# Tile-by-tile halves, a longer head step and moved splits in a transformer kernel in fp32

## The chip, the core and the metric

The kernel runs on one core of one Trainium2 chip. The metric is the device time of one execution in microseconds (us). Engines: PE is TensorE (matmuls and transposes), DVE is VectorE, ACT is ScalarE, POOL is GpSimd, SP is SyncE, which issues the weight loads. Each engine has its own queue and works through it strictly in order; semaphores tie the queues together.

## What is computed

Two transformer layers follow one another on 256 tokens of width 2048, all in fp32:

```python
# first layer: mixer, cross attention, feed-forward
h = rmsnorm(x, g); dq, dk, dv, rq, rk, rv, rg = split_cols(h @ w_in)
da = rmsnorm(diff_attention(dq, dk, dv, lam, slopes)) * (1 - lam_init)   # 4 heads
ret = rmsnorm(retention(rq, rk, rv)) * silu(rg)
x = x + concat(da, ret) @ w_o
xo = softmax((rmsnorm(x) @ w_xq) (rmsnorm(mem) @ w_xk)^T / sqrt(512)) @ (rmsnorm(mem) @ w_xv)   # 4 heads
x = x + xo @ w_xo
hf = rmsnorm(x);  x = x + (silu(hf @ w_gate) * (hf @ w_up)) @ w_down
x = rmsnorm(x, norm_f_g)
# second layer: modulated input, windowed GQA and pooling branches, gated merge
shift, scale, gate = split(silu(c) @ w_ada + b_ada)
h = rmsnorm(x) * (1 + scale) + shift
q, k, v, gate_a, u, gate_p = split(h @ w_in_2)
merged = g_a * (y_a @ w_branch_attn) + g_p * (y_p @ w_branch_pool)
out = x + gate * rmsnorm(merged @ w_out)
```

## The kernel before

**Operands.** Tokens stand in two tiles of 128 (tile 0 and tile 1). Each fp32 factor is split into a high and a low part in fp32r, and each product is three matmuls, high by high, high by low and low by high, of 128 rows by 512 columns (L1069 to L1071). Weights come in *half panels*: 256 rows by 512 columns, in SBUF as 128 x 1024 numbers. SP loads one into one of eight raw places, ACT makes its high part whi (L1604), DVE its low part wlo (L2334: raw minus whi). Both lie in a ring of four slots (HALVES), slot n % 4. A *step* of the stream is one half panel met with one tile (6 matmuls) or with both (12). Panels are computed in pairs, whose first chunk is done with seven products in the manner of Strassen (M1 to M7); this needs sums of raw halves (L2347) and sums of activations, the *forms* (fah, fal, fbh, fbl).

**Order.** The class Stream lists the steps of the whole program; each of the four programs (tensor, scalar, vector, gpsimd) goes through the same list. Ahead of each step ACT and DVE make the parts of the halves up to `made`, which is four past the last half that has been met; after it a queue of *jobs*, Python generators, goes on by one `yield` of its first job. So the order of the other work (attention heads, norms, splits of activations) against the matmuls is written out by these yields and by `pause(n)`.

**Differential heads.** On TensorE a head is scores (L704, L705), then a turn of the probabilities and probabilities times v (L719 to L721), which end in bank A[0]. ACT squares the result (L1100), DVE makes the mean (L1653), POOL the root (L2389), and DVE scales the result (L1890). After the scale comes the next head's scores or, behind the pair's second head, the turn of the mixed rows (L648). One yield lies between the last matmul of a head and what follows it.

**hx3 and memory.** While w_o's last panels run, the memory rows are squared on ACT (mem_stats, L1100, eight squares in four steps), and hx3, the last chunk of the cross attention's input, is turned by TensorE (L648) and split (ACT L1113, DVE L1674).

**xq and xo.** The cross heads wait for c_p (DVE) and for turned copies (L1758, L1181). The forms of xo are built by DVE (L1703 to L1706, L1710) and ACT (L1157) while xq's last panels run. L1165 on ACT scales a panel's rows by a root before TensorE turns them (L648).

**e3 and kv.** e3 is the last panel of the last down projection, with six halves: the first two are met with both tiles, the last four with tile 0 and then with tile 1 ("last"), so that tile 0's sum is complete four halves before tile 1's. kv is the first panel of the second layer, with eight: its first four halves are met with tile 0, then tile 1, and the last four with both ("first"). In between stands the final norm: for each tile DVE adds the residual (L2050), multiplies by the gain (L2052), makes the mean (L2054 to L2062); ACT makes two squares (L1100); POOL makes the roots (L2389). Then each chunk j of tile t is scaled by the root (scale_chunk: DVE L2043 for even j, ACT L1374 for odd), turned by TensorE (L836), modulated by scale and shift (ACT L1407, DVE L2085), and split (ACT L1413, DVE L2090). kv's eight low parts are made not by DVE but by POOL (low_parts, L2406), counted by the semaphore lo_pool. The chunks come in the order (0,0), (1,0) behind tile 0 and (0,1), (1,1), (2,0), (2,1), (3,0), (3,1) behind tile 1, each in banks ps4 and ps5.

## Time and profile before

| | |
|---|---|
| median of 3 runs | 2101.16 us (2100.3 to 2101.31) |
| profiled execution, its own time | 2102.25 us |
| its span, first to last instruction | 2100.5 us |
| mean granted TensorE clock | 0.997 |
| PE busy | 2062.7 us (98%) |
| DVE busy | 1678.4 us (80%) |
| ACT busy | 1175.9 us (56%) |
| POOL busy | 73.0 us (3%) |

A row of a timeline gives start, length, engine, line, operation and shape, and in brackets how long the engine had been idle and what released it. Matmuls overlap, since the next one is issued before the last has ended; what a matmul costs is read from start to start, not from its length. The page's idle time is the end of one to the start of the next, so an excess from start to start is some 0.15 us more than the idle time in brackets.

### The profile page before, as it was taken

The page shows a single profiled execution, that of the slowest core. Times are in us where ns is not written, and L with a number is a line of the kernel's source. Part 1 is how long each engine was busy: PE and PEld are TensorE (multiplying, and loading weights), DVE is VectorE, ACT ScalarE, POOL GpSimd, SP SyncE. Part 2 cuts the span into 40 slices and gives each one's busy share as a digit, 9 for nine tenths or more (in the row PEclk, how much of TensorE's full clock was granted, in tenths as well). Part 3 has the DMA queues.
Part 4 walks back from the last instruction along what each step waited for, and adds up shares of the span by engine and source line. Part 5 has one row for each costly group of instructions (what it writes and reads, how often), then busy time and mean ns, then how long its engine had stood idle before and what let it go on. Part 6 is the DMA issues. An engine that isn't in the chain of part 4 may idle for free.

```text
span 2100.5 us, 25386 instructions
## 1 busy us (share of the span) xinstructions
PE 2062.7 (98%) x9334; PEld 1700.3 (81%) x9334; DVE 1678.4 (80%) x1839; ACT 1175.9 (56%) x1522; POOL 73.0 (3%) x94
## 2 busy tenths in 40 slices
PE   9999999999999999999999999999899999999998
PEld 8887888788887888888888888888678888888786
DVE  6777778876765788998889898898688768988875
ACT  7665556755654565555555555555656655654453
POOL 1000000000000000000000000000310000000000
PEclk9999999999999999999999999999999999999999
DMA  9555557565544458777777777776465566889653
GB/s 343 171 177 170 184 172 261 188 200 179 189 161 150 140 191 289 255 262 248 235 239 256 264 240 248 234 275 204 125 208 181 181 191 226 266 290 325 222 198 107
DMA packets 218955, 453.75 MB, mean 216 GB/s; under 512 B 14400, under 2 KB 16592, under 8 KB 218704
## 3 DMA queue, kind: packets, MB, share of 16 engines
q1 hardware_dynamic: 212928, 432.07, 61.4%
q0 software_dynamic: 5616, 19.94, 3.0%
q8 instruction: 74, 1.21, 0.2%
q14 instruction: 49, 0.40, 0.1%
q10 hardware_dynamic: 288, 0.13, 0.0%
HBM read 447.88 MB, written 4.19 MB: 215 GB/s over the span
## 4 chain that ended last, share of the span: by engine, by line
PE 85%; issue 7%; DVE 5%; ACT 2%; DMA 1%; POOL 0%; DVEq 0%; ACTq 0%; POOLq 0%
PE ps L1069 26%; PE ps L1071 26%; PE ps L1070 26%; DVE wlo L2334 2%; PE ps L648 2%; PE ps L778 1%; PE ps L798 1%; ACT whi L1604 0%; ACT junk L1100 0%; PE ps L884 0%; DMA FR<-in_mem_dram 0%; PE ps L926 0%; PE ps L915 0%; PE ps L864 0%; DVE raw L2347 0%
## 5 line engine op out<-in xcount | busy, mean ns | idle before, releaser
L2334 DVE TENSOR_TENSOR wlo<-raw,whi 128x1024 fp32r<-128x1024 f32 x832 | 1006.0, 1220 | 261.1 <-ACT whi L1604 254.0
L1604 ACT ACTIVATE whi<-raw 128x1024 fp32r<-128x1024 f32 x840 | 882.2, 1058 | 592.6 <-PE ps L1071 545.9
L1069 PE MATMUL ps<-whi,ah 128*128 128x512 f32 x1618 | 642.6, 397 | 7.9 <-DVE wlo L2334 4.1
L1071 PE MATMUL ps<-whi,al 128*128 128x512 f32 x1618 | 631.7, 390 | 0.0
L1070 PE MATMUL ps<-wlo,ah 128*128 128x512 f32 x1618 | 630.7, 390 | 0.0
L1069 PEld LDWEIGHTS ps<-whi,ah 128*128 128x128 f32 x1618 | 304.5, 188 | 72.6 <-issue 6.9
L1071 PEld LDWEIGHTS ps<-whi,al 128*128 128x128 f32 x1618 | 304.1, 188 | 64.8
L1070 PEld LDWEIGHTS ps<-wlo,ah 128*128 128x128 f32 x1618 | 304.7, 188 | 61.2 <-issue 0.2
L1069 PE MATMUL ps<-whi,bh 128*128 128x512 f32 x862 | 341.2, 396 | 5.7 <-DVE wlo L2334 4.0
L1071 PE MATMUL ps<-whi,bl 128*128 128x512 f32 x862 | 336.1, 390 | 0.0
L1070 PE MATMUL ps<-wlo,bh 128*128 128x512 f32 x862 | 335.6, 389 | 0.0
L2347 DVE TENSOR_TENSOR raw<-raw 128x1024 f32<-128x1024 f32 x160 | 197.9, 1237 | 26.7 <-DVE wlo L2334 26.7
L1069 PEld LDWEIGHTS ps<-whi,bh 128*128 128x128 f32 x862 | 161.9, 188 | 41.6 <-issue 4.6
L1071 PEld LDWEIGHTS ps<-whi,bl 128*128 128x128 f32 x862 | 161.8, 188 | 34.3
L1070 PEld LDWEIGHTS ps<-wlo,bh 128*128 128x128 f32 x862 | 162.0, 188 | 33.5 <-issue 1.0
L1985 DVE SCALAR_TENSOR_TENSOR FR<-raw,Z,FR 128x1024 f32<-128x1024 f32 x90 | 115.0, 1278 | 0.0
L1069 PE MATMUL ps<-whi,fah 128*128 128x512 f32 x208 | 84.0, 404 | 0.5 <-DVE fal L1710 0.5
L1071 PE MATMUL ps<-whi,fal 128*128 128x512 f32 x208 | 81.2, 390 | 0.0
L1070 PE MATMUL ps<-wlo,fah 128*128 128x512 f32 x208 | 81.1, 390 | 0.0
L1176 ACT ACTIVATE side<-ps 128x512 f32<-128x512 f32 x120 | 70.8, 590 | 17.7 <-PE ps L1071 17.7
L2389 POOL TENSOR_TENSOR Z<-Z 128x2 f32<-128x2 f32 (+1 forms) x18 | 13.1, 729 | 1443.5 <-DVE Z L1653 770.4
L1715 DVE TENSOR_TENSOR FR<-ps,side 128x512 f32<-128x512 f32 x81 | 53.1, 683 | 7.5 <-PE ps L1071 7.5
(237 smaller groups left out, 1340.3 us busy)
## 6 DMA issues: line engine op xcount, KB each, us to landing
raw<-in_w_in_dram SPq DMA_DIRECT2D x168, 512.0 KB, 4.5
raw<-in_w_ada_dram SPq DMA_DIRECT2D x96, 512.0 KB, 4.7
raw<-in_w_gate_dram SPq DMA_DIRECT2D x88, 512.0 KB, 4.9
raw<-in_w_up_dram SPq DMA_DIRECT2D x88, 512.0 KB, 5.2
raw<-in_w_down_dram SPq DMA_DIRECT2D x88, 512.0 KB, 5.3
raw<-in_w_merge_dram SPq DMA_DIRECT2D x64, 512.0 KB, 5.1
raw<-in_w_o_dram SPq DMA_DIRECT2D x32, 512.0 KB, 4.8
raw<-in_w_xk_dram SPq DMA_DIRECT2D x32, 512.0 KB, 4.7
```

What stands on the lines that cost most here:

```text
L648: ins = e.transpose(T[b].ap[:, kk * 256 + t * 128:kk * 256 + t * 128 + 128], src[:, t, (2 * b + kk) * 128:(2 * b + kk + 1) * 128], ident[: ...
L778: ins = e.matmul(A[0].ap[:, t * S:(t + 1) * S], QTC[:, d, t * 128:(t + 1) * 128], XKT[:, 4 * h + d, :], start=(d == 0), stop=(d == 3))
L798: ins = e.matmul(A[b].ap[:, dd * S:(dd + 1) * S], XV[:, k, c0:c0 + 128], PTC[:, k, :], start=(k == 0), stop=(k == 1))
L1069: e.matmul(o, xh[:, k, tokens], wh, start=first, stop=False, skip_group_check=more)
L1070: e.matmul(o, xh[:, k, tokens], wl, start=False, stop=False, skip_group_check=more)
L1071: ins = e.matmul(o, xl[:, k, tokens], wh, start=False, skip_group_check=more, stop=kk == 1 and (st.end or st.form in READ))
L1176: done(e.activation(side_of(pair[place[0]], place[1]), bank_of(pair[panel], t)[:, :], ACT.Copy), "snap")
L1604: done(e.activation(whi[:, n % HALVES, :], place(item), ACT.Copy), "hi")
L1715: return e.tensor_tensor(dst, src, side_of(p, t), side_op(p))
L1985: done(e.scalar_tensor_tensor(acc, src, csilu[:, k:k + 1], acc, ALU.mult, ALU.add), "ada")
L2334: done(e.tensor_tensor(wlo[:, n % HALVES, :], src, whi[:, n % HALVES, :].bitcast(F32), ALU.subtract), "lo")
L2347: done(e.tensor_tensor(place(item), place(add), place(item), ALU.subtract if minus else ALU.add), "t_sum")
```

## The change

Four parts.

1. e3 and kv are met tile by tile in six halves each instead of four: all of e3's six by tile, kv's first six by tile and its last two with both. A ring of four cannot hold six, so two halves lie aside: e3's first two in the places of chunks 2 and 3 of activations that are free then, kv's first two in the places of the forms. `_slots` works out the slot of each half, what it waits for, and `made`. POOL's low parts go to DVE, and lo_pool is gone. The chunks come as (0,0), (1,0), (2,0), (0,1), (1,1), (2,1), (3,1), (3,0), by turns in the banks T (ps4, ps5) and A (ps6, ps7); (0,0) and (1,0) are turned while e3 still runs for tile 1. On ACT and DVE a job second_input does tile 0's chunks, tile 1's gain product and squares, and then the rest, with a chunk's high and low parts one step behind its modulation from (0,1) on. The sum for M5 of the pair behind kv comes one half nearer to its use.
2. diff_head has one more yield on TensorE, ACT and DVE at its end.
3. hx3 is split before the last memory squares: on ACT after the second of the four steps of squares, on DVE after two pauses, on TensorE two steps earlier.
4. xo's forms take one step more on TensorE, ACT and DVE, and the third cross head pauses two steps instead of three ahead of its turn, as the fourth has done.

```diff
                 if c == 1 and panel.kind in ("ba", "bp"):
                     self._add_ada(self._late)
                 self._entry(self._item(p, c, hf))
-        if panel.stagger == "first":
-            self.pool_halves = range(base, base + n)
-        a, b = {"first": (0, HALVES), "last": (n - HALVES, n), None: (n, n)}[panel.stagger]
+        for h, at in {("e", 3): ((0, ("a", 2)), (1, ("a", 3))),
+                      ("kv", 0): ((0, "forms_a"), (1, "forms_b"))}.get((panel.kind, panel.i), ()):
+            self.aside_at[base + h] = at
+        by_tile = HALVES + sum(base <= m for m in self.aside_at)
+        a, b = {"first": (0, by_tile), "last": (n - by_tile, n), None: (n, n)}[panel.stagger]
...
+        early = 1 if self.panels[f - 1].stagger == "first" else 2
+        for form, n in (("M5", at["M5"] - early), ("M6", at["M3"] + 1), ("M7", at["M1"] + 2),
...
+        self.slot, self.slot_free, ring = {}, {}, []
+        for n in range(self.total):
+            if n in self.aside_at:
+                self.slot[n], self.slot_free[n] = self.aside_at[n], self.free[n]
+            else:
+                self.slot[n] = len(ring) % HALVES
+                self.slot_free[n] = ring[-HALVES] + 1 if len(ring) >= HALVES else 0
+                ring.append(n)
+        first_use = {}
+        for i, st in enumerate(self.steps):
+            first_use.setdefault(st.n, i)
+        met = made = 0
+        for i, st in enumerate(self.steps):
+            ahead = len(self.steps)
+            if len(st.tiles) == 1 and st.form is None:
+                ahead = HALVES if self.panels[st.p].kind == "out" else 3
+            while made < self.total and self.slot_free[made] <= met and (
+                    made in self.aside_at or first_use[made] <= i + ahead):
+                made += 1
+            self.steps[i] = st._replace(made=made)
+            if st.taken:
+                met = st.n + 1
...
+        mod_order = ((0, 0), (1, 0), (2, 0), (0, 1), (1, 1), (2, 1), (3, 1), (3, 0))
...
+        def mod_banks(j, t):
+            return A if mod_order.index((j, t)) % 2 else T
...
+        def split_at(n):
+            at_n = stream.slot[n]
+            if isinstance(at_n, int):
+                return whi[:, at_n, :], wlo[:, at_n, :]
+            if isinstance(at_n, tuple):
+                parts = [buf[:, 4 * at_n[1]:4 * at_n[1] + 4, :] for buf in at[at_n[0]]]
+            else:
+                parts = [buf[:, :, :] for buf in forms[at_n[-1]]]
+            return [part.rearrange("p a b -> p (a b)") for part in parts]
...
                 e.matmul(A[0].ap[:, 256:512], AAT[:, 256:384], vb[:, 1, cols], start=False,
                          stop=True).then_inc(A[0].full, 1)
                 yield
+                yield
...
-                for _ in range(3 if h < 3 else 2):
+                for _ in range(3 if h < 2 else 2):
...
+                        jobs.start(make_forms(3))
...
+                    if t == 0:
+                        jobs.start(pause(3))
+                        for j, tt in mod_order:
+                            jobs.start(modulated(j, tt))
+                            if (j, tt) in ((1, 0), (2, 0)):
+                                jobs.start(pause(2 if j == 1 else 1))
+                    else:
...
-                        jobs.start(pause(4))
+                        jobs.start(pause(2))
...
                     for t in range(2):
                         square(MT[j % 2][:, t, :], ss_m[:, 2 * j + t:2 * j + t + 1], "m_sq")
                     yield
+                    if j == 1:
+                        yield from turn_x("hx3", ("hx", 3), gcols("nx", 3))
...
+            def second_input():
+                yield from pause(3)
+                mod_sums(0, 0)
+                mod_high(0, 0)
+                yield
+                mod_sums(1, 0)
+                mod_high(1, 0)
+                yield
+                yield
+                gain_square(1)
+                yield
+                mod_sums(2, 0)
+                mod_high(2, 0)
+                yield
+                scale_chunk(1, 1)
+                yield
+                for i, (j, t) in enumerate(mod_order[3:]):
+                    for nj, nt in mod_order[5 + i:6 + i]:
+                        if nj % 2:
+                            scale_chunk(nj, nt)
+                    mod_sums(j, t)
+                    if i:
+                        mod_high(*mod_order[2 + i])
+                    yield
+                mod_high(*mod_order[-1])
...
                 elif kind == "e" and i < 3:
                     aside.start(down2(p, i))
                 elif kind == "e":
-                    last_down(p, t)
+                    down_square(p, t)
+                    if t == 0:
+                        gain_square(t)
+                        scale_chunk(1, t)
+                        jobs.start(second_input())
+                    else:
+                        jobs.start(make_forms("mod"))
+                        jobs.start(pause(4))
...
                         jobs.start(make_forms("mem"))
                     if c == 3:
                         jobs.start(mem_stats())
-                        jobs.start(turn_x("hx3", ("hx", 3), gcols("nx", 3)))
...
                 a11, a21, a12, a22 = (AF[name][:, 2 * k:2 * k + 2, t * P:(t + 1) * P] for k in range(2) for t in range(2))
                 after_own(done(e.tensor_tensor(a22, a21, a22, ALU.subtract)))
                 after_own(done(e.tensor_tensor(a21, a11, a21, ALU.subtract)))
+                if name == "xo":
+                    yield
...
                 yield
             def mem_stats():
-                for _ in range(4):
-                    yield
+                yield from pause(2)
+                yield from to_stationary("hx3", ("hx", 3), gcols("nx", 3))
+                yield from pause(2)
                 e.wait_ge(s["m_sq"], 8)
...
+            def mod_low(j, t):
                 e.wait_ge(s["mod_hi"], mod_order.index((j, t)) + 1)
                 hi, lo = (part[:, :, t * P:(t + 1) * P] for part in hi_lo(("mod", j)))
-                done(e.tensor_tensor(lo, tmp, hi.bitcast(F32), ALU.subtract), f"mod{t}")
+                done(e.tensor_tensor(lo, tmp_of(j, t), hi.bitcast(F32), ALU.subtract), f"mod{t}")
+            def second_input(p):
+                yield from pause(3)
+                scale_chunk(2, 0)
+                mod_sums(0, 0)
+                yield
+                mod_low(0, 0)
+                mod_sums(1, 0)
+                yield
+                mod_low(1, 0)
+                yield
+                down_gain(p, 1)
+                yield
+                down_mean(1)
+                mod_sums(2, 0)
+                mod_low(2, 0)
+                yield
+                scale_chunk(0, 1)
+                yield
+                for i, (j, t) in enumerate(mod_order[3:]):
+                    for nj, nt in mod_order[5 + i:6 + i]:
+                        if nj % 2 == 0:
+                            scale_chunk(nj, nt)
+                    mod_sums(j, t)
+                    if i:
+                        mod_low(*mod_order[2 + i])
+                    yield
+                mod_low(*mod_order[-1])
...
-            def low_parts(upto):
-                while made[0] < upto:
-                    n = stream.pool_halves[made[0]]
-                    made[0] += 1
-                    src = place(stream.entries[n].item)
-                    e.wait_ge(s["hi"], n + 1)
-                    e.tensor_tensor(wlo[:, n % HALVES, :], src, whi[:, n % HALVES, :].bitcast(F32),
-                                    ALU.subtract).then_inc(s["lo_pool"], 1)
...
             final_roots(0)
-            low_parts(4)
             final_roots(1)
-            low_parts(8)
```

In the excerpts below the names are those of the kernel's buffers: ps a PSUM bank, FR a scratch region, Z the small columns, X the residual, ah and al the high and low parts of activations. The lines of the changed kernel differ from those before: L1113 to L1115 are the three matmuls, L743 and L744 the scores, L1144 the square, L1157 the high split of a turned chunk, L1679 whi, L2440 wlo, L2127 and L2131 tile 1's sum and gain product, L2162 a modulated chunk's low part, L2155 its modulation, L2122 the scale by the root.

TensorE at the second pair of differential heads, before: six matmuls of the pair's forms product stand behind the head's L721 (just above), then come the scores of head 3.

```order
L1069 MATMUL ps<-whi,fah 128x512
L1070 MATMUL ps<-wlo,fah 128x512
L1071 MATMUL ps<-whi,fal 128x512
L704 MATMUL ps<-FR 128x128 [waits s_a0_free]
L705 MATMUL ps<-FR 128x256
L704 MATMUL ps<-FR 128x128 [waits s_a1_free]
L705 MATMUL ps<-FR 128x256
L1069 MATMUL ps<-whi,ah 128x512 [waits s_ev10,s_lo]
L1070 MATMUL ps<-wlo,ah 128x512
L1071 MATMUL ps<-whi,al 128x512
```

And after: the same six come first, and these six of the next step follow them ahead of the scores.

```order
L1113 MATMUL ps<-whi,ah 128x512 [waits s_ev10,s_lo]
L1114 MATMUL ps<-wlo,ah 128x512
L1115 MATMUL ps<-whi,al 128x512
L1113 MATMUL ps<-whi,ah 128x512
L1114 MATMUL ps<-wlo,ah 128x512
L1115 MATMUL ps<-whi,al 128x512
L743 MATMUL ps<-FR 128x128 [waits s_a0_free]
L744 MATMUL ps<-FR 128x256
L743 MATMUL ps<-FR 128x128 [waits s_a1_free]
L744 MATMUL ps<-FR 128x256
```

The scores moved by one step of 6 matmuls, from behind the product with fah to behind the next one.

ACT at the end of w_o, before: whi parts, the memory squares of chunks 2 and 3, and then hx3's high split.

```order
L1604 ACTIVATE whi<-raw 128x1024 [waits s_half,s_raw7]
L1100 ACTIVATE junk,Z<-FR 128x512 [waits s_m_sq,s_mt0]
L1100 ACTIVATE junk,Z<-FR 128x512 [waits s_m_sq]
L1604 ACTIVATE whi<-raw 128x1024 [waits s_half,s_t_sum]
L1100 ACTIVATE junk,Z<-FR 128x512 [waits s_m_sq,s_mt1]
L1100 ACTIVATE junk,Z<-FR 128x512 [waits s_m_sq]
L1604 ACTIVATE whi<-raw 128x1024 [waits s_half,s_raw2]
L1113 ACTIVATE ah<-ps,G 128x256 [waits s_half,s_t0_full]
L1113 ACTIVATE ah<-ps,G 128x256
```

And after: hx3's split (L1157) stands ahead of those squares.

```order
L1679 ACTIVATE whi<-raw 128x1024 [waits s_half,s_raw7]
L1157 ACTIVATE ah<-ps,G 128x256 [waits s_half,s_t0_full]
L1157 ACTIVATE ah<-ps,G 128x256
L1679 ACTIVATE whi<-raw 128x1024 [waits s_half,s_t_sum]
L1157 ACTIVATE ah<-ps,G 128x256 [waits s_t1_full]
L1157 ACTIVATE ah<-ps,G 128x256
L1679 ACTIVATE whi<-raw 128x1024 [waits s_half,s_raw2]
L1144 ACTIVATE junk,Z<-FR 128x512 [waits s_m_sq,s_mt0]
L1144 ACTIVATE junk,Z<-FR 128x512 [waits s_m_sq]
```

hx3's four pieces moved up by two steps and the squares of two chunks down by two.

DVE where e3's second tile ends, before: the low parts of chunks (0,0) and (1,0), then tile 1's sum, gain product and mean with no weight work in between (POOL has it).

```order
L2090 TENSOR_TENSOR al<-FR,ah 128x4x128 [waits s_mod_hi]
L2085 TENSOR_SCALAR FR<-ps,Z 128x128 [waits s_t1_full]
L2085 TENSOR_SCALAR FR<-ps,Z 128x128
L2090 TENSOR_TENSOR al<-FR,ah 128x4x128 [waits s_mod_hi]
L2050 TENSOR_TENSOR FR<-ps,X 128x512 [waits s_half]
L2052 TENSOR_TENSOR X<-FR 128x512 [waits s_ev11]
L2054 TENSOR_REDUCE Z<-Z 128x1 [waits s_sqg]
L2056 TENSOR_REDUCE Z<-Z 128x1 [waits s_sqf]
L2057 TENSOR_SCALAR Z<-Z 128x1 [waits s_dve]
L2058 SCALAR_TENSOR_TENSOR Z<-Z 128x1 [waits s_dve]
L2061 TENSOR_TENSOR Z<-Z 128x1 [waits s_sqg,s_dve]
L2062 TENSOR_SCALAR Z<-Z 128x1 [waits s_dve]
```

And after: weight low parts stand between the low part of (1,0), tile 1's sum and its gain product.

```order
L2440 TENSOR_TENSOR wlo<-raw,whi 128x1024 [waits s_hi]
L2162 TENSOR_TENSOR al<-FR,ah 128x4x128 [waits s_mod_hi]
L2127 TENSOR_TENSOR FR<-ps,X 128x512 [waits s_half]
L2440 TENSOR_TENSOR wlo<-raw,whi 128x1024 [waits s_hi]
L2131 TENSOR_TENSOR X<-FR 128x512 [waits s_ev11]
L2440 TENSOR_TENSOR wlo<-raw,whi 128x1024 [waits s_hi]
L2136 TENSOR_REDUCE Z<-Z 128x1 [waits s_sqg]
L2138 TENSOR_REDUCE Z<-Z 128x1 [waits s_sqf]
L2139 TENSOR_SCALAR Z<-Z 128x1 [waits s_dve]
L2140 SCALAR_TENSOR_TENSOR Z<-Z 128x1 [waits s_dve]
L2143 TENSOR_TENSOR Z<-Z 128x1 [waits s_sqg,s_dve]
L2144 TENSOR_SCALAR Z<-Z 128x1 [waits s_dve]
```

Behind the mean stand, in the changed order, a chunk of tile 0 and one more weight part, and then the scale of (0,1), the first L2122 here.

```order
L2155 TENSOR_SCALAR FR<-ps,Z 128x128 [waits s_t1_full]
L2155 TENSOR_SCALAR FR<-ps,Z 128x128
L2162 TENSOR_TENSOR al<-FR,ah 128x4x128 [waits s_mod_hi]
L2440 TENSOR_TENSOR wlo<-raw,whi 128x1024 [waits s_hi]
L2122 TENSOR_SCALAR FR<-X,Z 128x512 [waits s_r]
L2122 TENSOR_SCALAR FR<-X,Z 128x512 [waits s_a1_full,s_r]
L2155 TENSOR_SCALAR FR<-ps,Z 128x128 [waits s_a1_full]
```

Three, then four, low parts of weights moved in ahead of that scale, and so did the modulation of (2,0); before, the scale of (0,1) stood right behind the mean.

## Rows read from the trace of the kernel before

**Rows 1.** Waits of TensorE over the span: in all, times, longest (us).

```profile
PE ps L1069 <- POOL wlo L2406: 1.8, 2, 1.2
```

**Rows 2.** Timeline, TensorE, 655 to 660: start, us, engine, line, operation [idle before, releaser].

```profile
655.46 0.39 PE L1070 MATMUL ps<-wlo,ah 128*128 128x512 f32 x1
655.69 0.39 PE L1071 MATMUL ps<-whi,al 128*128 128x512 f32 x1
658.25 1.97 PE L648 MATMUL ps<-ident,FR 128*128 128x128 f32 x8 [2.18 <-ACT FR L1165]
```

**Rows 3.** Timeline, TensorE, at the heads and the turns behind them.

```profile
90.36 0.49 PE L704 MATMUL ps<-FR 128*128 128x128 f32 x2 [0.24 <-DVE FR L1890]
...
165.09 0.49 PE L704 MATMUL ps<-FR 128*128 128x128 f32 x2 [1.58 <-DVE FR L1890]
...
182.21 0.66 PE L648 MATMUL ps<-ident,FR 128*128 128x128 f32 x4 [1.58 <-DVE FR L1890]
...
189.93 0.66 PE L648 MATMUL ps<-ident,FR 128*128 128x128 f32 x4 [1.09 <-ACT FR L1165]
```

**Rows 4.** Timeline, TensorE, at 416.

```profile
416.00 0.47 PE L1069 MATMUL ps<-whi,bh 128*128 128x512 f32 x1 [1.60 <-DVE wlo L2334]
```

**Rows 5.** Timeline, TensorE, from the end of e3 into kv.

```profile
1496.36 0.63 PE L836 MATMUL ps<-ident,FR 128*128 128x128 f32 x4 [0.82 <-issue]
1497.70 0.50 PE L1069 MATMUL ps<-whi,ah 128*128 128x512 f32 x1 [0.71 <-DVE al L2090]
...
1507.07 0.66 PE L836 MATMUL ps<-ident,FR 128*128 128x128 f32 x4 [2.60 <-DVE FR L2043]
...
1508.44 0.63 PE L1069 MATMUL ps<-whi,ah 128*128 128x512 f32 x1
1508.87 0.63 PE L1070 MATMUL ps<-wlo,ah 128*128 128x512 f32 x1
...
1509.72 1.05 PE L836 MATMUL ps<-ident,FR 128*128 128x128 f32 x4
```

**Rows 6.** Timeline, TensorE, after kv, in the q pair.

```profile
1533.17 0.50 PE L1069 MATMUL ps<-whi,fah 128*128 128x512 f32 x1 [0.46 <-DVE fal L1710]
...
1537.45 0.47 PE L1069 MATMUL ps<-whi,ah 128*128 128x512 f32 x1 [1.27 <-DVE wlo L2334]
```

**Rows 7.** Timeline, VectorE, before the scores at 165.09.

```profile
164.16 0.88 DVE L1890 TENSOR_SCALAR FR<-ps,Z 128x256 f32<-128x256 f32 x2 [0.80 <-POOL Z L2389]
```

**Rows 8.** Timeline, ScalarE, at the memory squares.

```profile
409.74 0.63 ACT L1100 ACTIVATE junk<-FR 128x512 bf16<-128x512 f32 x1 [3.84 <-DMA FR<-in_mem_dram]
```

**Rows 9.** Timeline, GpSimd, in kv.

```profile
1494.70 10.78 POOL L2406 TENSOR_TENSOR wlo<-raw,whi 128x1024 fp32r<-128x1024 f32 x4 [1.23 <-ACT whi L1604]
```

**Rows 10.** Timeline, VectorE, 1501 to 1508.

```profile
1501.09 2.15 DVE L2052 TENSOR_TENSOR X<-FR 128x512 f32<-128x512 f32 x1
...
1503.59 1.90 DVE L2058 SCALAR_TENSOR_TENSOR Z<-Z 128x1 f32<-128x1 f32 x1
...
1507.77 0.73 DVE L2085 TENSOR_SCALAR FR<-ps,Z 128x128 f32<-128x128 f32 x2 [0.36 <-PE ps L836]
```

**Rows 11.** Page, part 5: count | busy us, mean ns | idle before.

```profile
L2334 DVE TENSOR_TENSOR wlo<-raw,whi 128x1024 fp32r<-128x1024 f32 x832 | 1006.0, 1220 | 261.1 <-ACT whi L1604 254.0
L1604 ACT ACTIVATE whi<-raw 128x1024 fp32r<-128x1024 f32 x840 | 882.2, 1058 | 592.6 <-PE ps L1071 545.9
```

**Rows 12.** Groups of VectorE, 1478 to 1550: count | busy us, mean ns.

```profile
L2043 DVE TENSOR_SCALAR FR<-X,Z 128x512 f32<-128x512 f32 x4 | 1.8, 484 | 1.3 <-POOL Z L2389 1.3
L2050 DVE TENSOR_TENSOR FR<-ps,X 128x512 f32<-128x512 f32 x2 | 1.4, 686 | 1.7 <-PE ps L1071 1.7
```

**Rows 13.** Groups of ScalarE, 1478 to 1550: count | busy us, mean ns.

```profile
L1413 ACT ACTIVATE ah<-FR 128x512 fp32r<-128x512 f32 x8 | 5.1, 631 | 4.6 <-issue 3.7 <-ACT FR L1407 0.7
```

**Rows 14.** Windows: length, busy us and count by engine, PEclk, DMA share, GB/s.

```profile
656.00:662.00 6.00, 3.82 (x15) 3.37 (x15) 4.24 (x6) 2.88 (x4) 0.00 (x0) 0.72 0.53 175
1520.00:1550.00 30.00, 26.62 (x116) 20.73 (x115) 28.60 (x32) 17.25 (x22) 10.26 (x11) 1.00 0.55 173
```

167 lines of the change are left out of this document (70 added, 97 removed).

## Prediction

> **What bounds the kernel now.** I read the busy times first: TensorE works in 98% of the span, and its work is 8400 matmuls of 512 columns that the change neither adds to nor removes. So only the time in which TensorE stands still, or runs at a low clock, can move. Second I read its waits over the whole span [rows 1] and third, in its timeline, each place where one start follows the last by more than the work explains. Fed without a break, a 512-column matmul starts every 0.23 us (655.46 to 655.69) [rows 2], so a half panel met with one tile (6 matmuls) is 1.36 us and with both tiles 2.72 us. The change touches places that together hold about 25 us of such excess. These are the places:
> - pair 0 and 1 of the differential heads: gaps of 0.24, 1.58, 1.58 and 1.09 us [rows 3], in starts an excess of 0.40, 1.75, 1.75 and 1.25 us;
> - 416.00, TensorE idle 1.60 us for a low part [rows 4];
> - 658.25, idle 2.18 us [rows 2];
> - the stretch from the down projection's last panel (e3) to the first of the second layer (kv), with eleven waits from 1496.36 to 1548.08 that sum to 12.6 us in starts, the first two, the largest and two of the last in [rows 5, 6], and a low clock after the largest.
>
> Of the clock, rows show this: after the 2.60 us of idle before 1507.07 the matmuls at 1508.44 and 1508.87 stand 0.43 apart, its lower level (1.2 GHz; at 2.4 GHz 0.23), until about 1511.4, which costs about 2 us [rows 5]. After the 2.18 us before 658.25 [rows 2] the mean granted clock of 656 to 662 is 0.72 [rows 14], which costs about 1.6 us. After gaps of 1.6 us it doesn't.
>
> **Differential heads.** One more step between the heads' last matmul and the means puts the scores of the next head, or the turn of the result, behind 12 matmuls and not 6 (at mix 0: 12 and not 24, since there the head ends one step later while the turn stays). The chain behind is fixed: square, mean, root, then DVE's two L1890 (0.88 us) [rows 7]. Where 6 matmuls left 1.75 us, 12 leave 1.75 - 1.36 = 0.40. By place: 90.36 loses its 0.40, mix 0 gains a new 0.40; 165.09 goes from 1.75 to 0.40; 182.21 now has 24 matmuls ahead and loses 1.75; 189.93 loses 1.25. Net **-4.35 us**. Bounds: -3.6 if the new gap at mix 0 is as large as the one now at 189.93, -5.1 if the 0.40s aren't there. The added step queues no DMA and each engine's rows between are whi and wlo parts with slack at that point.
>
> **hx3 ahead of the memory squares.** At 416.00 DVE's low part is late because ACT's high part is, and ACT stood still 3.84 us at 409.74 for the memory rows' DMA [rows 8], then did two squares per step. With the split of hx3 (two 0.42 us pieces and no DMA behind it) in front and squares later, the high part for that step comes without two squares (4 instructions, 1.5 us) ahead of it. The 1.85 us goes: **-1.85 us**, bounds -2.2 (with the wait's shadow after it) and -1.0 (if the split, whose transposes PE makes at 413.80, is itself late by the step that was saved). The memory mean comes later too, but its root is first read when xk is scaled, a panel on; if that weren't so, the cost would be a step's wait there, which is within the bound of -1.0.
>
> **xq and xo.** The forms of xo take one step more on each engine and the third cross head pauses one less, so that the turn of its panel stands one step later. At 658.25 TensorE waits for ACT's L1165, which waits behind DVE's forms and L1715 in the order. A step more is 2.72 us, more than the 2.18 idle. The wait (2.34 in starts) and the low clock after it (1.6) go, less a slack of 0.15 that is missing on the c_p link: **-3.8 us**. Bounds: -2.3 if a smaller idle time still lowers the clock, -3.9 in full.
>
> **e3 and kv.** Here more is exchanged than saved, and it decides the size of the result. Now: POOL makes kv's eight low parts, four in 10.78 us [rows 9], and TensorE waits for two of them, 1.8 us [rows 1]; beside them the product of tile 1 with the gain takes 2.15 us (an undisturbed one of its shape 0.69 [rows 12]) and a one-column instruction 1.90 [rows 10], some 7 us of lengthening in all up to 1530. After: DVE makes them, 8 x 1.22 = 9.8 us more [rows 11], and gets the 7 back. I walked the order of the changed kernel with undisturbed durations: low part 1.22, high part 1.06 (0.95 apart), sum or product of 512 columns 0.69, scale 0.48 [rows 12], square 0.63 [rows 8] and its read 0.19, ScalarE's high part of a chunk 0.63 [rows 13], half a chunk's modulation 0.73 [rows 10].
> - Tile 0's sum comes three us earlier (1486.3 and not 1489.3), because six halves are met tile by tile; both first chunks are then turned inside tile 1's matmuls. The waits at 1496.36 and 1497.70 (0.99 + 0.96) go. kv starts at 1495.6 and not 1497.7, and its first two halves lie ready.
> - Then DVE and ACT work in strict turns, each step needing the other's last: half 2's high part to 1497.0, its low part to 1498.25 (TensorE waits 0.4), chunk (1,0)'s low part to 1498.9, tile 1's sum to 1499.5, its square, half 3's high part to 1501.2, its low part to 1502.45: TensorE, which needs it at 1500.2, waits **2.2**. The gain product to 1503.05, its square, half 4's parts to 1504.8 and 1506.0, the mean's six small rows to 1507.0, chunk (2,0)'s sums, high and low part to 1509.2, half 5's low part to 1510.65, and only then the scale of chunk (0,1), to 1511.1. TensorE has finished half 3 at 1503.9 and stands **7.2 us**; a low clock of about 1.7 follows, as at 1507.07.
> - So (0,1) is turned at 1511.1, not 1507.07: 4.0 us later, with one half (1.36) and one chunk's turn (0.41) more already done. From there to the first step of the q pair, before 78 matmuls (17.7), six turns (2.5), low clock (2.0), waits (3.8): 26.1, the row at 1533.17 [rows 6]. After: 72 matmuls (16.4), five turns (2.1), low clock (1.7), waits (1.1): 21.2, so about 1532.3. DVE's lighter work after it takes another 0.4 off the waits at 1537.45 and 1548.08 [rows 6].
>
> Net **-1.3 us**; bounds +2 (each of the nine hand-overs 0.3 longer than the bare rows) and -6 (whi and wlo parts overlapping better than my walk). What POOL held up on DVE is taken as gone in full because the last lengthened instruction, a one-column one from 1503.59 on, ended at 1505.49 as POOL's fourth did at 1505.48 [rows 9, 10]. The Trainium skill, SBUF — State Buffer, section "Who interferes with whom", says that a DVE instruction with two SBUF inputs and a GpSimd instruction reading SBUF take turns on an exclusive port pair, and the loser blocks; by it nothing of the lengthening can stay, and if another cause held it (the loads landing) up to 2 us of the 7 would remain on DVE at 1521. The Trainium skill, Perfetto Trace Analysis, section "Optimizing Scalar/DVE Operations", would speak against the move, since there DVE is the busy one: 28.60 of 30 us in 1520 to 1550 [rows 14]; by it the sum would be worse by at most 9.8 - 7 = 2.8 us, which takes -1.3 to +1.5, inside the bounds.
>
> **The sum.** -4.35 - 1.85 - 3.8 - 1.3 = -11.3 us against the profiled execution's 2102.25, so 2090.95. That execution lies 1.09 above the median 2101.16; the same for the changed kernel gives **2089.9 us**. What a measurement can tell from no change is 0.2%, 4.2 us: 2097.0 and 2105.4 are the bounds of "same".
>
> **Rivals.**
> - *The turns between DVE and ACT don't bind.* If high parts run ahead (ACT is idle much of 1496 to 1511) and my strict order is wrong about which row waits, the 7.2 us stall and its low clock shrink to nothing: 2089.9 - 8.9 = 2081. Against it: each wait stands in the changed order.
> - *A step later is a step too late.* In heads, hx3 or xo the moved work meets the next deadline: one gap like 658.25's with its low clock (3.9) comes back, or hx3 pays its full 1.85 and the head gaps half: 2094 to 2097. For it: the 2.72 step covers xo's gap by only 0.5 us.
> - *Slower: tile 1's chunks go at round-trip pace.* After (0,1), four more chunk turns stand between half panels, one every 6 matmuls (1.77 us with the turn). A chunk's round (modulation 0.73, low part 0.69, scale 0.48, ACT's high part 0.63, the low part of a half 1.22) is 3.75 us, with hand-overs 4.0, if nothing of it overlaps, which gives 4 x 2.2 = 8.9 us of waits, and TensorE, idle more than half of it, would keep its lower level for the 48 matmuls that kv meets by tile from there (48 x 0.2 - 1.7 = 7.9 more): 2089.9 + 8.9 + 7.9 = 2106.7. It decides from a round of 3.7 us with that clock, of 5.6 without. Against it: banks alternate in twos and the rows 1507.07 to 1512 show two such turns 2.65 apart [rows 5].
> - *POOL's work was free and DVE's isn't* is the 2.8 us above, within the forecast.
>
> **Chances.** Forecast (2086 to 2094) 0.60; turns don't bind (2079 to 2086) 0.14; step too late (2094 to 2098) 0.21, a quarter of it within 0.2%; slower 0.03; the rest, 0.02, in between. So faster 0.90, same 0.07, slower 0.03. The range reaches from the first rival's 2081 to 2096, which leaves out about 0.05 below and 0.1 above.
>
> **What would show it.** In the profile after: no idle at 164 to 190 above 0.5 us; none at the step after hx3's turn; at xo no low clock; no POOL tensor work at e3; the gain product of tile 1 at 0.69; tile 0's end three us earlier against the kernel's start of e3; a 2 us wait at kv's half 3 and a wait of about 7 us for DVE's scale at the turn of (0,1), with slow matmuls after. Wrong would be the forecast if that last wait is under 4 us, or if any second one above 2 us follows.

## The result and the profile after

The changed kernel takes **2090.92 us** (median of 5 runs, 2090.46 to 2090.99) against 2100.58 us for the kernel before (5 runs, 2100.12 to 2101.31): 9.66 us less, a ratio of 0.9953 with a 95% interval of 0.9938 to 0.9967, so 7 to 13 us. The forecast was 2089.9 us, which was 11.3 us less than the median before. The profiled execution took 2090.46 us, 11.8 less than the profiled one before.

First part 1 of the changed kernel's page: busy time, share of the span and count of instructions by engine. POOL's work fell from 73.0 to 53.4 us, and DVE's stayed at 1678, although it took over eight low parts.

```profile
span 2088.3 us, 25390 instructions
...
PE 2058.2 (99%) x9334; PEld 1699.1 (81%) x9334; DVE 1678.3 (80%) x1847; ACT 1175.1 (56%) x1522; POOL 53.4 (3%) x86
```

TensorE runs the same 9334 instructions in both kernels, so the two traces can be laid over each other: the start of the same place in TensorE's queue, after minus before. The third column is what each stretch changed. Each trace is one execution.

| place (start in the trace before) | after - before, us | stretch | forecast |
|---|---|---|---|
| 84, ahead of the heads | -0.36 | -0.36 | 0 |
| 264, behind the heads | -4.89 | -4.53 | -4.35 |
| 403, ahead of the memory squares | -4.92 | -0.03 | 0 |
| 423, behind hx3 | -6.35 | -1.43 | -1.85 |
| 631, ahead of the cross heads | -6.37 | -0.02 | 0 |
| 711, behind xo's first turn | -10.30 | -3.93 | -3.8 |
| 1478, start of e3 | -10.21 | +0.09 | 0 |
| 1548, in the q pair | -11.44 | -1.23 | -1.3 |
| 1982 | -11.48 | -0.04 | 0 |
| 1990, last panels | -12.05 | -0.57 | 0 |

Two of these stretches, the first and the last, don't belong to the change, as the second profile of the kernel before shows below.

Three places in TensorE's timeline of the changed kernel: the turn at mix 0, the scores at head 3 (165.09 in [rows 3]) and the turn behind hx3. In brackets: idle time and releaser.

```profile
116.15 0.66 PE L688 MATMUL ps<-ident,FR 128*128 128x128 f32 x4 [0.21 <-DVE FR L1967]
...
164.66 0.49 PE L743 MATMUL ps<-FR 128*128 128x128 f32 x2 [0.21 <-DVE FR L1967]
...
416.87 0.66 PE L688 MATMUL ps<-ident,FR 128*128 128x128 f32 x4 [0.75 <-ACT FR L1211]
```

The new gap at mix 0 and the rest at head 3 are 0.21 us each (0.37 in starts, forecast 0.40). What stood at 90.36, 182.21 and 189.93 in [rows 3] is gone. At 416.87 a wait has grown: 0.91 in starts, where the trace before has 0.30.

TensorE's timeline of the changed kernel from kv's half 3 (1492.10) over the turn of chunk (0,1) (1500.51) to half 4, which answers to [rows 5]:

```profile
1492.10 0.50 PE L1113 MATMUL ps<-whi,ah 128*128 128x512 f32 x1 [1.90 <-DVE wlo L2440]
...
1500.51 1.11 PE L877 MATMUL ps<-ident,FR 128*128 128x128 f32 x4 [6.47 <-DVE FR L2122]
1501.28 0.78 PE L1113 MATMUL ps<-whi,ah 128*128 128x512 f32 x1
1501.85 0.63 PE L1114 MATMUL ps<-wlo,ah 128*128 128x512 f32 x1
1502.28 0.63 PE L1115 MATMUL ps<-whi,al 128*128 128x512 f32 x1
```

Both waits of the forecast are there: 2.07 us in starts (forecast 2.2) and 6.87 (7.2), and then matmuls 0.43 apart. VectorE's timeline beside it, from the low part of (1,0) to the scale of (0,1):

```profile
1487.80 0.68 DVE L2162 TENSOR_TENSOR al<-FR,ah 128x512 fp32r<-128x512 f32 x1
1488.40 0.68 DVE L2127 TENSOR_TENSOR FR<-ps,X 128x512 f32<-128x512 f32 x1
1490.82 1.22 DVE L2440 TENSOR_TENSOR wlo<-raw,whi 128x1024 fp32r<-128x1024 f32 x1 [1.74 <-ACT whi L1679]
1491.97 0.68 DVE L2131 TENSOR_TENSOR X<-FR 128x512 f32<-128x512 f32 x1
1494.39 1.23 DVE L2440 TENSOR_TENSOR wlo<-raw,whi 128x1024 fp32r<-128x1024 f32 x1 [1.74 <-ACT whi L1679]
...
1496.42 0.72 DVE L2155 TENSOR_SCALAR FR<-ps,Z 128x128 f32<-128x128 f32 x2
1497.89 0.69 DVE L2162 TENSOR_TENSOR al<-FR,ah 128x512 fp32r<-128x512 f32 x1 [0.74 <-ACT ah L1453]
1498.83 1.23 DVE L2440 TENSOR_TENSOR wlo<-raw,whi 128x1024 fp32r<-128x1024 f32 x1 [0.25 <-ACT whi L1679]
1499.97 0.88 DVE L2122 TENSOR_SCALAR FR<-X,Z 128x512 f32<-128x512 f32 x2
```

And ScalarE's, at the same time (L1144 is tile 1's square, L1679 the high part of a half):

```profile
1489.12 0.63 ACT L1144 ACTIVATE junk<-FR 128x512 bf16<-128x512 f32 x1 [2.50 <-DVE FR L2127]
...
1489.75 1.04 ACT L1679 ACTIVATE whi<-raw 128x1024 fp32r<-128x1024 f32 x1
1492.68 0.63 ACT L1144 ACTIVATE junk<-X 128x512 bf16<-128x512 f32 x1 [1.89 <-DVE X L2131]
...
1493.31 1.04 ACT L1679 ACTIVATE whi<-raw 128x1024 fp32r<-128x1024 f32 x1
```

Read the brackets of both from top to bottom. Twice DVE stands 1.74 us for a high part of ACT, and ACT had stood 2.50 and 1.89 us for the row of DVE just above (the sum, then the gain product), on which its square waits; the high part stands behind the square. In the 12.2 us from 1487.80 to 1499.97 DVE is idle 4.5, and both of TensorE's waits end on a row of DVE. The gain product takes 0.68 us, where [rows 10] had 2.15.

### The profile page after: what moved, and what is told of

Its sections match the earlier page's. It is cut to its first block and busy times, and to the rows that moved or that the text cites. A ratio compares the mean times of both kernels' runs of the same rounds, so it can differ in the third digit from the quotient of the medians.

```text
span 2088.3 us, 25390 instructions
## 1 busy us (share of the span) xinstructions
PE 2058.2 (99%) x9334; PEld 1699.1 (81%) x9334; DVE 1678.3 (80%) x1847; ACT 1175.1 (56%) x1522; POOL 53.4 (3%) x86
## 5 line engine op out<-in xcount | busy, mean ns | idle before, releaser
L2440 DVE TENSOR_TENSOR wlo<-raw,whi 128x1024 fp32r<-128x1024 f32 x836 | 1010.9, 1221 | 258.1 <-ACT whi L1679 250.9
L1679 ACT ACTIVATE whi<-raw 128x1024 fp32r<-128x1024 f32 x836 | 877.9, 1058 | 583.7 <-PE ps L1115 541.1
L1113 PE MATMUL ps<-whi,ah 128*128 128x512 f32 x1610 | 638.7, 397 | 6.7 <-DVE wlo L2440 6.5
L1115 PE MATMUL ps<-whi,al 128*128 128x512 f32 x1610 | 628.2, 390 | 0.0
L1113 PEld LDWEIGHTS ps<-whi,ah 128*128 128x128 f32 x1610 | 302.7, 188 | 70.3 <-DVE wlo L2440 5.1
L1115 PEld LDWEIGHTS ps<-whi,al 128*128 128x128 f32 x1610 | 302.5, 188 | 64.4
L1113 PE MATMUL ps<-whi,bh 128*128 128x512 f32 x854 | 337.9, 396 | 4.1 <-DVE wlo L2440 2.4
L1115 PE MATMUL ps<-whi,bl 128*128 128x512 f32 x854 | 332.9, 390 | 0.0
L1113 PEld LDWEIGHTS ps<-whi,bh 128*128 128x128 f32 x854 | 160.4, 188 | 38.6 <-issue 4.9
L1115 PEld LDWEIGHTS ps<-whi,bl 128*128 128x128 f32 x854 | 160.3, 188 | 34.1
L1113 PE MATMUL ps<-whi,fah 128*128 128x512 f32 x208 | 84.0, 404 | 0.0
L1115 PE MATMUL ps<-whi,fal 128*128 128x512 f32 x208 | 81.2, 390 | 0.0
```

The lines of the kernel that those rows point to most:

```text
L1113: e.matmul(o, xh[:, k, tokens], wh, start=first, stop=False, skip_group_check=more)
L1115: ins = e.matmul(o, xl[:, k, tokens], wh, start=False, skip_group_check=more, stop=kk == 1 and (st.end or st.form in READ))
L1679: done(e.activation(split_at(n)[0], place(item), ACT.Copy), "hi")
L2440: done(e.tensor_tensor(lo, place(stream.entries[n].item), hi.bitcast(F32), ALU.subtract), "lo")
```

## The experiments

**Each part alone.** Four kernels hold one part of the change each. The heads:

```diff
                 e.matmul(A[0].ap[:, 256:512], AAT[:, 256:384], vb[:, 1, cols], start=False,
                          stop=True).then_inc(A[0].full, 1)
                 yield
+                yield
...
                     square(A[0].ap[:, q * 256:q * 256 + 256], ss_d[h][:, q:q + 1], "d_sq")
                 yield
+                yield
...
                                           root_col[f"d{h}"][:, q:q + 1], None, ALU.mult)
                 ins.then_inc(A[0].free, 1)
                 yield
+                yield
```

> The kernel before with one more yield at the end of each differential head on TensorE, ACT and DVE, and nothing else. If the four waits at the heads and turns behave as summed: -4.35 us against the kernel before (-3.6 to -5.1). Rival, that the moved scores only meet the next deadline: -1 to -2.5.

Measured: 2096.02 us (10 runs) beside 2100.17 (31 runs of the kernel before on the same chip), 4.15 less, ratio 0.9981 (0.9972 to 0.9991). In its trace the stretch from 84 to 264 is 4.6 us shorter. The added step does what the sum said.

hx3 alone (first TensorE's pause, then ACT, then DVE):

```diff
                     if c == 3:
-                        jobs.start(pause(4))
+                        jobs.start(pause(2))
...
                     yield
+                    if j == 1:
+                        yield from turn_x("hx3", ("hx", 3), gcols("nx", 3))
...
                         jobs.start(mem_stats())
-                        jobs.start(turn_x("hx3", ("hx", 3), gcols("nx", 3)))
...
             def mem_stats():
-                for _ in range(4):
-                    yield
+                yield from pause(2)
+                yield from to_stationary("hx3", ("hx", 3), gcols("nx", 3))
+                yield from pause(2)
...
                         jobs.start(mem_stats())
-                        jobs.start(to_stationary("hx3", ("hx", 3), gcols("nx", 3)))
```

> The kernel before with only hx3's split ahead of the last memory squares. As summed: -1.85 us. The trace of the changed kernel holds a new wait of 0.91 in starts where 0.30 was, at the turn at 416.87: if that is this part's doing, -1.4. Rival: the new wait comes from another part, then -1.85.

Measured: 2099.31 us, 0.86 less, ratio 0.9993 (0.9984 to 1.0002), which isn't clear of no change by its interval. Its trace is 1.4 us shorter between 403 and 423 and has the wait of 0.90 at the turn (421.41). So that wait is this part's doing, the first of the two cases expected: ACT's scale for the turn stands behind DVE's rows, and the step that was saved brings TensorE there earlier.

xq and xo alone (excerpt: ACT has the same shorter pause, and DVE one at its c_p loop):

```diff
-            def make_forms():
-                yield
-                yield
+            def make_forms(steps=2):
+                yield from pause(steps)
...
-                for _ in range(3 if h < 3 else 2):
+                for _ in range(3 if h < 2 else 2):
...
                     if i == 1:
-                        jobs.start(make_forms())
+                        jobs.start(make_forms(3))
...
                     done(ins, "af")
                 yield
+                if name == "xo":
+                    yield
```

> The kernel before with only the extra step of xo's forms and the third cross head's shorter pause. -3.8 us, of which about 2.3 is the wait at 658.25 and 1.6 the low clock behind it. Rival, that a shorter wait stays and still lowers the clock: -2.3 or less.

Measured: 2097.15 us, 3.02 less, ratio 0.9988 (0.9978 to 0.9997), so 0.6 to 4.6 us: between the two, and the interval holds both. Its trace against the trace before is 3.90 shorter from 631 to 711, as in the changed kernel. What can make the median give less is shown further down. The extra step and the shorter pause were not taken apart.

e3 and kv alone, which is the changed kernel with the other three parts put back:

> The changed kernel without its other three parts: only e3 and kv in six halves by tile, low parts on DVE, chunks in the new order. -1.3 us against the kernel before (+2 to -6). If the parts are independent, the four runs add up to the whole change's -9.7.

Measured: 2100.3 us, 0.13 more, ratio 0.9998 (0.9989 to 1.0007). So the median shows no gain from the largest part of the diff. Its trace repeats both waits (2.05 and 6.9 us in starts). The four runs add up to 7.9 us and not 9.7; the difference lies inside their intervals and isn't explained further.

**What makes the wait of 6.87 us.** Four kernels move work on DVE and ACT in the stretch around it. The kernels before that ran beside them have medians of 2100.57 and 2100.35, the one beside the changed kernel 2100.58, so differences from the changed kernel below 0.3 us mean nothing. The first changes DVE's order only:

```diff
                 down_mean(1)
+                scale_chunk(0, 1)
                 mod_sums(2, 0)
                 mod_low(2, 0)
                 yield
-                scale_chunk(0, 1)
                 yield
```

> The changed kernel with DVE's scale of chunk (0,1) directly behind tile 1's mean, ahead of the modulation of (2,0) and of half 5's low part. If DVE's order is what TensorE waits for at that turn (6.87 us in starts), the turn comes 2.4 us sooner and a new wait of about 1.5 us for the low part of (2,0) follows at half 4: -0.5 to -2 us against the changed kernel, 2089 to 2090.4. Rival, that what counts is the sum of DVE's work and not its order: no change, 2090.9.

Measured: 2090.29 us (2090.01 to 2090.79, 4 runs; the kernel before beside it 2100.57), 0.6 less than the changed kernel's 2090.92. TensorE's timeline:

```profile
1497.76 0.69 PE L877 MATMUL ps<-ident,FR 128*128 128x128 f32 x4 [3.93 <-DVE FR L2122]
...
1499.83 0.79 PE L1113 MATMUL ps<-whi,ah 128*128 128x512 f32 x1 [1.39 <-DVE al L2162]
```

The turn comes 2.75 us sooner. About half of that is given back at once, at half 4, to the low part of (2,0), which now ends last: 1.66 in starts. Nearly all of the rest goes to the clock. Behind that wait it is low until 1505.08, over ten matmuls and a turn; behind the long wait of the changed kernel it is low over one turn and five matmuls.

```profile
1502.00:1505.00 3.00, 3.00 (x10) 2.41 (x10) 1.45 (x4) 1.78 (x4) 0.00 (x0) 0.50 0.65 175
```

The turn two further on starts at 1505.57, and at 1505.63 in the changed kernel. From e3's start to 1548 the two traces differ by 0.2 us, so of the 0.6 us between the medians no more than that is seen in them. DVE's order is what TensorE waits for at that turn, but one row alone only moves the wait on.

The second gives tile 1's norm to DVE and ACT in one piece:

```diff
 # DVE, where tile 1's sum stands
                     else:
+                        down_gain(p, 1)
+                        down_mean(1)
                         jobs.start(make_forms("mod"))
...
 # DVE, second_input
-                down_gain(p, 1)
-                yield
-                down_mean(1)
-                mod_sums(2, 0)
-                mod_low(2, 0)
-                yield
                 scale_chunk(0, 1)
+                mod_sums(2, 0)
+                yield
+                mod_low(2, 0)
+                yield
                 yield
...
 # ACT, where tile 1's square stands
                     else:
+                        gain_square(1)
                         jobs.start(make_forms("mod"))
...
 # ACT, second_input
-                gain_square(1)
-                yield
                 mod_sums(2, 0)
+                yield
                 mod_high(2, 0)
-                yield
                 scale_chunk(1, 1)
                 yield
+                yield
```

> The changed kernel with tile 1's norm in one piece: on DVE sum, gain product and mean without weight low parts in between, on ACT both squares together, and the scale of (0,1) and the modulation of (2,0) one step sooner. If the strict turns between ACT and DVE make the long wait: the wait at half 3 grows from 2.1 to 2.8, the one of 6.87 at the turn of (0,1) goes with the low clock behind it, and one of about 1.2 comes at half 4: -6.5 us against the changed kernel, about 2084.4 (2083 to 2087). Rival, that ACT's and DVE's total work bounds this stretch: within 1 us of 2090.9.

Measured: **2084.54 us** (2084.45 to 2084.73, 4 runs), 6.4 us less than the changed kernel, ratio to the kernel before 0.9925 (0.9908 to 0.9941). Its TensorE timeline over the same places:

```profile
1492.99 0.50 PE L1113 MATMUL ps<-whi,ah 128*128 128x512 f32 x1 [2.73 <-DVE wlo L2440]
...
1494.64 1.06 PE L877 MATMUL ps<-ident,FR 128*128 128x128 f32 x4
1495.76 0.79 PE L1113 MATMUL ps<-whi,ah 128*128 128x512 f32 x1
```

The turn of (0,1) follows half 3 without a wait, at 1494.64 and not 1500.51. This settles the cause: the same instructions, no fewer on any engine, in another order. The total came out as expected, but two of its terms did not: the low clock did not go (3.4 us of it from 1494.29 on, behind the longer wait at half 3), and the wait expected at half 4 was 0.35 us in starts and not 1.2. How much of the 6.4 us is due to the norm in one piece and how much to the scale and modulation one step sooner was not taken apart; the kernel above shows that the sooner scale alone brings almost nothing.

The third lets the parts of halves met by tile be made up to four steps ahead, on top of the second:

```diff
-                ahead = HALVES if self.panels[st.p].kind == "out" else 3
+                ahead = HALVES
```

> The changed kernel with tile 1's norm in one piece and, besides, ScalarE's and VectorE's parts of halves met by tile made up to four steps ahead instead of three. If DVE's work in 1484 to 1497 is what bounds now: within 1 us of the version with the norm in one piece (2084.5), a smaller wait at half 3 and a new one of 2 to 3 at the turn of (0,1). Rival, that the late high parts of ACT are the bound: 2082 or less.

Measured: 2087.77 us (2086.48 to 2088.39, 4 runs), 3.2 us worse than without it, so neither side was right. Its waits by the timeline:

```profile
1486.70 0.51 PE L1113 MATMUL ps<-fah,ah 128*128 128x512 f32 x1 [1.12 <-DVE al L2162]
...
1490.86 0.50 PE L1113 MATMUL ps<-whi,ah 128*128 128x512 f32 x1 [0.72 <-DVE al L2162]
...
1495.64 0.66 PE L877 MATMUL ps<-ident,FR 128*128 128x128 f32 x4 [1.76 <-DVE FR L2122]
...
1498.02 0.80 PE L1113 MATMUL ps<-whi,ah 128*128 128x512 f32 x1 [1.72 <-DVE al L2162]
```

I had looked at the waits from half 3 on only (the two lower rows, about 2 us each in starts) and had left out the upper two (1.30 and 0.97); half 3 itself has no wait any more. Low parts of weights that are made sooner stand in front of the chunks' own low parts, which TensorE needs first. And from 1498 to 1503 the granted clock is 0.50:

```profile
1498.00:1503.00 5.00, 4.98 (x14) 4.03 (x15) 1.96 (x6) 2.44 (x6) 0.00 (x0) 0.50 0.41 129
```

The last puts half 3's parts where both engines wait anyway, on top of the second:

```diff
 # ACT, ahead of tile 1's squares
+                    if t == 1:
+                        make(made + 1)
                     down_square(p, t)
...
 # DVE
                         down_gain(p, 1)
+                        make(made + 1)
                         down_mean(1)
...
-                scale_chunk(0, 1)
                 mod_sums(2, 0)
+                scale_chunk(0, 1)
```

> As the version with the norm in one piece, but half 3's high part goes ahead of tile 1's squares on ACT and its low part between the gain product and the mean on DVE. The wait at half 3 falls from 2.9 to about 0.9, one of about 1.2 comes at the turn of (0,1) and one of about 1.4 at half 4, since DVE is busy without a break from tile 1's sum on: 2084.0 (2083.3 to 2084.7). Rival, that only ACT's order counted: 2082.5.

Measured: **2082.79 us** (2082.68 to 2083.34, 4 runs), 17.6 us below the kernel before on that chip, ratio 0.9916 (0.9901 to 0.9931), and the best of all. TensorE's timeline, and two windows of 6 us (busy time by engine, then the granted clock), first of the version with the norm in one piece, then of this one:

```profile
1491.12 0.50 PE L1113 MATMUL ps<-whi,ah 128*128 128x512 f32 x1 [0.81 <-DVE wlo L2443]
...
1493.15 0.66 PE L877 MATMUL ps<-ident,FR 128*128 128x128 f32 x4 [0.38 <-DVE FR L2124]
...
1494.89 0.51 PE L1113 MATMUL ps<-whi,ah 128*128 128x512 f32 x1 [1.08 <-DVE al L2164]
```

```profile
1493.00:1499.00 6.00, 5.94 (x22) 4.55 (x23) 5.20 (x10) 4.27 (x9) 0.37 (x1) 0.72 0.66 183
```

```profile
1493.00:1499.00 6.00, 4.67 (x25) 3.59 (x25) 5.58 (x11) 5.38 (x12) 0.14 (x1) 1.00 0.70 209
```

The waits are 0.97, 0.54 and 1.32 us in starts, where I had said 0.9, 1.2 and 1.4. The time fell by 1.75 us and not 0.5. It lies below the range that I had given and nearer to the rival's 2082.5, but the rival's reason does not hold: all three waits left end on a row of DVE, which is busy without a break from 1488.52 to 1497.80. The waits together are 0.4 us shorter than with the norm in one piece. What I had left out of the sum is the low clock: TensorE's granted clock is 1.00 after an idle time of 0.81 us, where it was 0.72 after one of 2.73. The mean granted clock is 0.999 in all four runs here and 0.998 in all four there. What is left of waits here is bounded by DVE's work.

**POOL's low parts on DVE, in the kernel before.** Only this is changed:

```diff
-        if panel.stagger == "first":
-            self.pool_halves = range(base, base + n)
...
             final_roots(0)
-            low_parts(4)
             final_roots(1)
-            low_parts(8)
```

> The kernel before with kv's eight low parts on DVE and nothing else changed. If POOL's reads hold DVE up, the gain product of tile 1 falls from 2.15 to 0.69, the one-column row from 1.90 to 0.16, the sum of raw halves from 3.41 to 1.22 and the form row from 2.61 to 0.42, and the time falls by 0 to 4 us although DVE has 9.8 us more work. Rival, that these rows are long for another reason (loads landing): they stay long and the time rises by 2 to 6 us.

Measured: 2101.58 us (10 runs) beside 2100.57, ratio 1.0004 (0.9995 to 1.0013). The groups of DVE in 1488 to 1550, with count, busy us and mean ns:

```profile
L2345 DVE TENSOR_TENSOR raw<-raw 128x1024 f32<-128x1024 f32 x4 | 4.9, 1221 | 0.4 <-DVE wlo L2332 0.4
...
L2050 DVE TENSOR_TENSOR X<-FR 128x512 f32<-128x512 f32 x2 | 1.4, 691 | 0.1
...
L1702 DVE TENSOR_TENSOR FR<-FR 128x256 f32<-128x256 f32 x1 | 0.4, 426 | 0.0
...
L2056 DVE SCALAR_TENSOR_TENSOR Z<-Z 128x1 f32<-128x1 f32 x2 | 0.3, 158 | 0.1
```

All four kinds are back at 1.22, 0.69, 0.43 and 0.16 us, from 3.41, 2.15, 2.61 and 1.90. POOL's eight low parts were the cause; the loads were not (their DMA share in 1488 to 1550 is 0.44, and 0.42 before). But the time did not fall, though I had expected it to, nor did it rise as the rival had it. The DVE rows are shorter, and there are 9.8 us more of them, so that tile 1's sum starts 25.9 us after e3's first step and not 22.3. Both waits for POOL go (1.8 us), and in their place TensorE's wait at the turn of (1,0) grows from 0.82 us (1496.36 in [rows 5]) to 2.27, with a low clock behind it that the trace before does not have:

```profile
1496.05 0.63 PE L834 MATMUL ps<-ident,FR 128*128 128x128 f32 x4 [2.27 <-DVE FR L2083]
```

The wait at the turn of (0,1) is 2.88 us (2.60 in [rows 5]), again with a low clock. For the time it is the same, to within the interval of 1 us less to 2.7 us more, whether POOL or DVE does this work.

**The kernel before, once more.** 

> The kernel before, unchanged, profiled a second time. Asked is whether the low clock behind the 2.18 us of idle before xo belongs to the kernel or comes and goes: four traces with the same wait left standing show a granted clock of 1.00 there. If it comes and goes, this profile shows 1.00 or the low value, and one left with it shows the start of the next stage 1.6 us sooner; then the median value of xo's part is 2.3 and not 3.9. If it belongs to the kernel: 0.7 to 0.8 over 654 to 662 again.

Measured: 2100.82 us (10 runs, 2099.05 to 2105.0), the same as before. Windows of its trace and of the trace shown before, over the wait ahead of xo. First the trace shown before, then the second one:

```profile
654.00:662.00 8.00, 5.82 (x24) 4.75 (x23) 6.24 (x7) 4.74 (x6) 0.00 (x0) 0.79 0.51 170
```

```profile
654.00:662.00 8.00, 5.82 (x23) 4.47 (x22) 6.48 (x7) 3.76 (x5) 0.00 (x0) 0.79 0.42 140
```

And the same window in the kernel with hx3 alone, which leaves this wait as it was (2.18 idle, 2.34 in starts):

```profile
654.00:662.00 8.00, 5.82 (x31) 4.83 (x30) 5.67 (x7) 2.94 (x5) 0.00 (x0) 1.00 0.45 139
```

The low clock behind an idle time of 2.18 us comes in two traces of six (absent in the traces with the heads, hx3, and e3 and kv alone, and with POOL's work moved). Where it is absent, the stretch from 631 to 711 is 1.6 us shorter. Behind the 2.60 us of [rows 5] it comes in one trace of five (absent with the heads, hx3 and xq alone); in the second trace of the kernel before the window behind it has 1.00.

```profile
1506.00:1512.00 6.00, 5.30 (x28) 4.31 (x29) 4.04 (x10) 4.21 (x9) 0.23 (x1) 1.00 0.24 83
```

Without it the stretch from e3's start to 1548 is only 0.6 us shorter, since a wait of 0.69 for a chunk's low part takes its place. The second trace is also 0.3 us shorter ahead of 84, 0.7 at the memory squares, and 0.58 in the last panels, where the first had a wait of 0.38 (at 1988.13) that the second has not.

## Why the prediction was right, and where it was off

- **The time** (2090.92, forecast 2089.9) lies in the range of 2081 to 2096, and the change was faster, as given 9 in 10. The gain was put at 11.3 and is 9.66. The sum counts two low clocks in full, 1.6 us at xo and about 2 behind 1507.07, that most other traces of the same waits do not have. That fits a forecast which is 1.6 us too large, but isn't shown.
- **Heads.** Forecast -4.35; -4.53 by the traces, -4.15 alone. The gap of 1.75 us at 165.09 became 0.37 (1.75 less the step's 1.36 is 0.39), so the chain behind a head kept its length and the step in front shortened the wait by just its own time.
- **hx3.** Forecast -1.85, bounds -1.0 to -2.2; -1.43 by the traces, -0.86 alone (+0.4 to -3.4 by its interval). What was mis-sized is "the 1.85 us goes", with nothing put in its place: a wait at the turn grew from 0.30 to 0.91, and in the second trace of the kernel before the wait that is saved is 1.10 and not 1.85, since the memory rows land sooner there (the first memory square starts at 408.15 and not 409.74).
- **xq and xo.** Forecast -3.8, bounds -2.3 and -3.9. The two traces differ by -3.93, but the median of this part alone is -3.0. The mis-sized term is the low clock of 1.6 us, taken in full from one profile; it is in two traces of six. An estimate with a third of it is 2.3 + 0.5 = 2.8. The traces show that it comes and goes; that this is what makes the median smaller is not shown, as its interval (0.6 to 4.6) holds 3.8 too. I had named the bound without it for another reason (that it stays), and not seen that it could be absent already.
- **e3 and kv.** Forecast -1.3; -1.23 by the traces, +0.1 alone with an interval of about 2 us to either side. The walk of the changed order held: waits of 2.07 and 6.87 for 2.2 and 7.2, the sum of tile 0 2.9 us earlier. What was too large is the other side of the balance, the low clock of 2.0 us behind 1507.07. By its own starts from 1508.02 to 1511.43 it cost 1.6, and in the four traces without it the kernel before is 0.6 us faster there, so the term becomes -0.6 in the changed kernel's trace and -0.3 in that of this part alone. The low clock of the changed kernel was expected behind the long wait; it had set in ahead of it.
- **The base.** I took the profiled execution as 1.09 above its median; over five runs it is 1.67. With 1.67 the forecast would have been 2089.3 and not 2089.9, further from the 2090.92 measured; the gain of 11.3 would be the same. The second trace, which is 1.9 us shorter, shows at which places such an excess stands, and two of the sum's terms (hx3, and the low clocks) were read at them.
- **The rivals.** "The turns don't bind" is ruled out by the trace (6.47 us idle for DVE's scale), and the version with the norm in one piece shows what another order was worth: 6.4 us, and 8.1 with half 3's parts moved too. "A step later is a step too late" came in a small form only, at hx3's turn. The round-trip rival did not come: the next two turns are at 1503.79 and 1505.63 with no wait. Its 7.9 us for a clock that stays low through such waits has no run here to bear it out.
- **POOL's work.** That nothing of the lengthening would stay was right: the gain product takes 0.68 us in the changed kernel. The Trainium skill, SBUF — State Buffer, section "Who interferes with whom", says that a DVE instruction with two SBUF inputs contends with a GpSimd instruction that reads SBUF. The traces agree: 2.15 us beside POOL's work, 0.69 without it. That the move costs up to 2.8 us was a bound; the kernel with it alone has a ratio of 1.0004. The Trainium skill, Perfetto Trace Analysis, section "Optimizing Scalar/DVE Operations", says that such an offload may make sense where DVE is saturated, but might not help since the two engines share a read port. The second half is borne out: moving the work to POOL is worth nothing that the ratio shows.

## What to carry to other kernels

Walk the order that a change makes, engine by engine with durations from the trace, up to the instruction for which the bounding engine waits; it gave both new waits here within 0.4 us, and showed ahead of any run that the largest part of the diff would bring little. Where two engines take turns for one result, keep its steps together and put other work where both wait anyway. Before a sum counts a low clock or a wait on a DMA, see whether a second profile of the same kernel has it.
